# A two-layer hybrid decoder trunk: layer 1 loads its input in runs of 32 features and turns it in 32 by 32 blocks on VectorE

## The reference, cut to what matters

```python
def _rmsnorm(x, w):
    return x * lax.rsqrt(jnp.mean(x * x, axis=-1, keepdims=True) + EPS) * w

def _layer(x, ...):
    h = _rmsnorm(x, norm_w)
    z = jnp.einsum('btd,dc->btc', h, w_in)      # 1024 -> 3088 columns
    ...                                         # GLA and retention, per head norm, SiLU gates
    return x + jnp.einsum('btc,cd->btd', mixed, w_out), ...

for l in range(2):
    hp = _layer(hp, ...)                        # the prompt
y_prompt = _rmsnorm(hp, final_norm_w)
```

## Time and profile before

| | |
|---|---|
| median of 3 runs | 1725.38 us |
| the profiled execution's own time | 1724.93 us |
| its span | 1722.9 us |
| TensorE busy | 1701.6 us, 99% of the span |
| VectorE, ScalarE, GpSimd busy | 55%, 38%, 49% |
| DMA queues: ScalarE's (q10), SyncE's (q1) | 23.7%, 14.2% of 16 engines |
| granted TensorE clock | full over the span (0.999) |

### The profile page before, as it was taken

The page is one execution under the profiler, slowest core; times in us unless marked ns, Lnnn a source line. Parts: engine busy times, 40 slices in busy tenths (PEclk is TensorE's granted clock), DMA queues, the critical chain, the costliest instruction groups (busy, mean ns, idle before and its releaser), DMA issues.

```text
span 1722.9 us, 26529 instructions
## 1 busy us (share of the span) xinstructions
PE 1701.6 (99%) x10266; PEld 1401.0 (81%) x10266; DVE 942.0 (55%) x2284; ACT 657.6 (38%) x1287; POOL 842.1 (49%) x661
## 2 busy tenths in 40 slices
PE   6999999999999999999999999999999999999998
PEld 4888878888788887888878888788888888878886
DVE  7643566746555174464454535759556464584454
ACT  4433334333344234343452424434244343443322
POOL 4444345654455444464444544547445464454635
PEclk9999999999999999999999999999999999999999
DMA  7422356434442244322452224563244322442224
GB/s 259 135 65 84 100 207 197 147 111 145 161 137 84 86 135 159 117 86 83 136 168 88 74 74 149 184 178 128 74 150 159 111 76 85 134 157 80 86 86 140
DMA packets 100189, 215.97 MB, mean 125 GB/s; under 512 B 12896, under 2 KB 15328, under 8 KB 100064
## 3 DMA queue, kind: packets, MB, share of 16 engines
q10 hardware_dynamic: 73872, 134.51, 23.7%
q1 hardware_dynamic: 26192, 79.76, 14.2%
HBM read 192.34 MB, written 21.89 MB: 124 GB/s over the span
## 4 chain that ended last, share of the span: by engine, by line
PE 99%; DMA 1%; DVE 0%; issue 0%; ACT 0%; ACTq 0%; POOLq 0%; POOL 0%; SPq 0%
PE bank L697 82%; PE bank L972 2%; PE bank L1013 2%; PE bank L978 2%; PE bank L760 1%; PE bank L956 1%; PE bank L939 1%; PE bank L918 1%; PE bank L373 1%; PE bank L880 1%; PE bank L922 1%; PE bank L718 0%; PE bank L989 0%; PE bank L770 0%; PE bank L897 0%; PE bank L662 0%
## 5 line engine op out<-in xcount | busy, mean ns | idle before, releaser
L264 POOL TENSOR_TENSOR w_lo<-w_stage,w_hi 128x512 fp32r<-128x512 f32 x264 | 360.9, 1388 | 352.3 <-ACT w_hi L257 352.3
L697 PE MATMUL bank<-h_hi,w_hi 128*128 128x512 f32 x1024 | 410.2, 401 | 3.7 <-DVE h_lo L361 3.7
L697 PE MATMUL bank<-h_lo,w_hi 128*128 128x512 f32 x1024 | 400.4, 391 | 0.0
L697 PE MATMUL bank<-h_hi,w_lo 128*128 128x512 f32 x1024 | 400.2, 391 | 0.0
L264 POOL TENSOR_TENSOR w_lo<-ss,w_hi 128x512 fp32r<-128x512 f32 x164 | 216.5, 1341 | 232.4 <-ACT w_hi L257 232.4
L257 ACT ACTIVATE w_hi<-w_stage 128x512 fp32r<-128x512 f32 x264 | 152.6, 624 | 352.4 <-PE bank L697 311.0
L697 PEld LDWEIGHTS bank<-h_hi,w_hi 128*128 128x128 f32 x1024 | 192.7, 188 | 53.9 <-issue 7.2
L697 PEld LDWEIGHTS bank<-h_hi,w_lo 128*128 128x128 f32 x1024 | 192.8, 188 | 41.5
L697 PEld LDWEIGHTS bank<-h_lo,w_hi 128*128 128x128 f32 x1024 | 193.0, 189 | 37.0
L697 PE MATMUL bank<-w_hi,m_hi 128*128 128x512 f32 x512 | 203.6, 398 | 0.0
L697 PE MATMUL bank<-w_hi,h_hi 128*128 128x512 f32 x512 | 202.7, 396 | 0.0
(11 more groups left out here) (221 smaller groups left out, 2279.8 us busy)
## 6 DMA issues: line engine op xcount, KB each, us to landing
w_stage<-in_w_slots ACTq DMA_DIRECT2D x264, 256.0 KB, 3.0
ss<-in_w_slots ACTq DMA_DIRECT2D x164, 256.0 KB, 2.9
v_b<-in_w_slots ACTq DMA_DIRECT2D x84, 256.0 KB, 3.0
region<-in_x_prompt SPq DMA_DIRECT2D x32, 512.0 KB, 4.2
xn<-in_x_t SPq DMA_DIRECT2D x16, 512.0 KB, 4.3
out_acts<-region SPq DMA_DIRECT2D x16, 512.0 KB, 3.5
xn<-out_acts SPq DMA_DIRECT2D x16, 512.0 KB, 3.8
region<-out_acts SPq DMA_DIRECT2D x16, 512.0 KB, 3.4
```

Of the source, the lines that this page charges most:

```text
L264: pool.tensor_tensor(w_lo[:, r, c], stage(h), w_hi[:, r, c].bitcast(f32), ALU.subtract).then_inc(lo_done, 1)
L697: i = pe.matmul(P[q][:, :], x, y, start=(s == 0 and kk == 0 and c == 0), stop=(s == 3 and kk == 1 and c == 2), skip_group_check=True)
```

## The change

Layer 1 gets its input in the layout of layer 0. The load of `acts` is cut: for each 128 features (k) and each 32 of them (j) one DMA brings 32 tokens by 16 groups by 32 features, so that partition 32j + b holds, for each of 16 groups of 32 tokens, token b's 32 features (runs of 128 bytes). 32 DMAs of 64 KB (8 in each of windows 4 to 7) stand where 4 of 512 KB stood. In window 20 VectorE turns all 32x32 blocks in place with 4 `transpose` instructions of 128x1024 (`next_turned`, in place of `next_norm`). The factors come from layer 0's output rows while they are in SBUF: the `tile_stats` and `mean_square` at the end of a block now run in layer 0 too (into `yvar`), GpSimd makes `xrs_1` of them in window 2 of the next block, and `next_stats` and its `rsqrt` in windows 18 and 19 are gone. `scale_rows`, `next_scaled` and the short forms of `next_hi` and `next_lo` are used in both layers; `next_transpose` is gone.

```diff
+        xrs_1, yvar = sb("xrs_1", [128, NBLK, TPB]), sb("yvar", [128, TPB])
+        xb_in = Count(sem("xb_in"), 512, base=-512 * NBLK)
...
-        def next_norm(vec, m):
-            vec.wait_ge(rstd_x.sem, rstd_x.at(m, 1))
-            for t in range(TPB):
-                i = vec.tensor_scalar(xn[:, t, :], xn[:, t, :], xrs[:, t:t + 1], None, ALU.mult)
+        def next_turned(vec, m):
+            vec.wait_ge(xb_in.sem, xb_in.at(m, 512))
+            for k in range(0, KT, 2):
+                i = vec.transpose(x_t[:, k:k + 2, :], x_t[:, k:k + 2, :])
             i.then_inc(xn_sb.sem, 1)
...
         def next_hi(act, m, k):
-            act.wait_ge(ht_ps.sem, ht_ps.at(m, k + 1))
-            h4 = xn[:, :, 128 * k:128 * k + 128]
-            nc.scalar.activation(h4, (X if k % 2 == 0 else ATT)..., ACT.Copy, scale=nw[:, k:k + 1]).then_inc(h_sb.sem, 1)
             act.wait_ge(h_sb.sem, h_sb.at(m, k + 1))
-            nc.scalar.activation(h_hi[:, k, :].rearrange(...), h4, ACT.Copy).then_inc(hhi_sb.sem, 1)
+            nc.scalar.activation(h_hi[:, k, :], x_t[:, k, :], ACT.Copy).then_inc(hhi_sb.sem, 1)
...
-        def next_transpose(pe, m, k):
-            ...
         def scale_rows(pe, m):
-            if m > 0:
+            factor = xrs if m < NBLK else xrs_1[:, m - NBLK, :]
+            if m >= NBLK:
+                pe.wait_ge(rstd_y.sem, rstd_y.at(m - NBLK, 1))
+            elif m > 0:
                 pe.wait_ge(rstd_x.sem, rstd_x.at(m, 1))
...
         def next_scaled(vec, m, k):
-                if m > 0:
+                if m >= NBLK:
+                    vec.wait_ge(xn_sb.sem, xn_sb.at(m, 1))
+                elif m > 0:
                     vec.wait_ge(x_in.sem, x_in.at(m, 64))
...
             def load_next(m, t):
-                    sp.dma_start(xn[:, t, :], d["acts"][c:c + TOK, :]).then_inc(x_in.sem, 16)
+                    for k in (2 * t, 2 * t + 1):
+                        runs = d["acts"][c:c + BLK, 128 * k:128 * k + 128].rearrange("(c b) (j a) -> j b c a", b=32, a=32)
+                        for j in range(4):
+                            sp.dma_start(x_t[32 * j:32 * j + 32, k, :].rearrange("p (c a) -> p c a", a=32), runs[j]).then_inc(xb_in.sem, 16)
...
-                        if w == (8 if n < NBLK - 1 else 19) and n < LAST:
+                        if w == 2 and 0 < n <= NBLK:                       # GpSimd
+                            pool.wait_ge(ystat.sem, ystat.at(n - 1, 4))
+                            rsqrt(xrs_1[:, n - 1, :], yvar[:, :], rstd_y.sem)
+                        if w == 8 and n < NBLK - 1:
...
-                        if w == 27 and n < NBLK - 1:                       # TensorE: scale_rows
+                        if w == 27 and n < LAST:
...
-                        if 27 <= w < 31 and NBLK - 1 <= n < LAST:
-                            for k in (2 * (w - 27), 2 * (w - 27) + 1):
-                                ...
-                                next_transpose(pe, n + 1, k)
...
-                        if w == (2 if n == 0 else 1 if n < NBLK - 1 else 18) and n < LAST:   # VectorE
+                        if w == (2 if n == 0 else 1) and n < NBLK - 1:
                             next_stats(vec, n + 1)
                         if w == 20 and NBLK - 1 <= n < LAST:
-                            next_norm(vec, n + 1)
+                            next_turned(vec, n + 1)
...
-                        if w == 28 and n < NBLK - 1:
+                        if w == 28 and n < LAST:
                             next_scaled(vec, n + 1, 0)
                             next_scaled(vec, n + 1, 1)
...
-                        if w == 30 and l == DEPTH - 1:
+                        if w == 30:
                             vec.wait_ge(y_add.sem, y_add.at(n, 4))
                             for t in range(TPB):
                                 tile_stats(vec, y_t, t, (0,))
...
-                        elif q > 0 and l == DEPTH - 1:
+                        elif q > 0:
                             vec.wait_ge(y_add.sem, y_add.at(n, 4 + q))
                             tile_stats(vec, y_t, q - 1, (1,))
...
-                    elif l == DEPTH - 1:
+                    else:
                         vec.wait_ge(y_add.sem, y_add.at(n, 8))
                         tile_stats(vec, y_t, TPB - 1, (1,)).then_inc(ystat.sem, 1)
-                        mean_square(vec, ystat, n % NBLK)
+                        mean_square(vec, ystat, n, xvar if l == DEPTH - 1 else yvar)
```

More of the change, by code:

```diff
@@ L286, in tile_stats, with mean_square @@
             return i
[L288 removed]
+        def mean_square(vec, count, n, var=xvar):
             vec.wait_ge(count.sem, count.at(n, 1))
@@ L297, in mean_square @@
             vec.wait_ge(count.sem, count.at(n, 3))
-            vec.scalar_tensor_tensor(xvar[:, :], xms[:, :], EPS, xagg[:, :, 1], ALU.add, ALU.add).then_inc(count.sem, 1)
+            vec.scalar_tensor_tensor(var[:, :], xms[:, :], EPS, xagg[:, :, 1], ALU.add, ALU.add).then_inc(count.sem, 1)
         def tile_mean_square(vec, s, t):
@@ L328, in next_stats @@
         def next_stats(vec, m):
[L329 to L332, removed]
+            vec.wait_ge(rows_in.sem, rows_in.at(m, 64))
             for t in range(TPB):
-                i = tile_stats(vec, x_rows if m < NBLK else xn, t)
+                i = tile_stats(vec, x_rows, t)
             i.then_inc(xstat.sem, 1)
             mean_square(vec, xstat, m)
-        def next_norm(vec, m):
-            vec.wait_ge(rstd_x.sem, rstd_x.at(m, 1))
-            for t in range(TPB):
-                i = vec.tensor_scalar(xn[:, t, :], xn[:, t, :], xrs[:, t:t + 1], None, ALU.mult)
+        def next_turned(vec, m):
+            vec.wait_ge(xb_in.sem, xb_in.at(m, 512))
+            for k in range(0, KT, 2):
+                i = vec.transpose(x_t[:, k:k + 2, :], x_t[:, k:k + 2, :])
             i.then_inc(xn_sb.sem, 1)
@@ L347, in next_hi @@
                 act.wait_ge(nw_in.sem, nw_in.at(m, 16))
[L348 to L351, removed]
-            act.wait_ge(ht_ps.sem, ht_ps.at(m, k + 1))
-            h4 = xn[:, :, 128 * k:128 * k + 128]
-            nc.scalar.activation(h4, (X if k % 2 == 0 else ATT)[:, :].rearrange("p (t n) -> p t n", t=TPB), ACT.Copy, scale=nw[:, k:k + 1]).then_inc(h_sb.sem, 1)
             act.wait_ge(h_sb.sem, h_sb.at(m, k + 1))
-            nc.scalar.activation(h_hi[:, k, :].rearrange("p (t n) -> p t n", t=TPB), h4, ACT.Copy).then_inc(hhi_sb.sem, 1)
+            nc.scalar.activation(h_hi[:, k, :], x_t[:, k, :], ACT.Copy).then_inc(hhi_sb.sem, 1)
         def next_lo(vec, m, k):
             vec.wait_ge(hhi_sb.sem, hhi_sb.at(m, k + 1))
[L360 to L364, removed]
-        def next_transpose(pe, m, k):
[L367 to L374, removed]
+            vec.tensor_tensor(h_lo[:, k, :], x_t[:, k, :], h_hi[:, k, :].bitcast(f32), ALU.subtract).then_inc(hlo_sb.sem, 1)
         def scale_rows(pe, m):
-            if m > 0:
+            factor = xrs if m < NBLK else xrs_1[:, m - NBLK, :]
+            if m >= NBLK:
+                pe.wait_ge(rstd_y.sem, rstd_y.at(m - NBLK, 1))
+            elif m > 0:
                 pe.wait_ge(rstd_x.sem, rstd_x.at(m, 1))
@@ L382, in scale_rows @@
                     pe.wait_ge(first_rs, t // 2 + 1)
-                i = pe.transpose(ATT[:, TOK * t:TOK * t + TOK], xrs[:, t:t + 1].to_broadcast([128, 128]), ident[:, :])
+                i = pe.transpose(ATT[:, TOK * t:TOK * t + TOK], factor[:, t:t + 1].to_broadcast([128, 128]), ident[:, :])
             i.then_inc(ht_ps.sem, KT)
@@ L405, in load_next @@
             def load_next(m, t):
-                c = m % NBLK * BLK + t * TOK
+                c = m % NBLK * BLK
                 if m < NBLK:
@@ L660, in hT_slot0 @@
                                 r = slice(64 * hf + 32 * (k % 2), 64 * hf + 32 * (k % 2) + 32)
[L661 to L664, removed]
+                                i = pe.matmul(ATT[r, 0:256], wg[:, k, :], x_t[:, k, 256 * hf:256 * hf + 256], start=(k < 2), stop=(k >= 6))
                         i.then_inc(slot_used, 1)
@@ L1761, in body @@
                                 vec.tensor_tensor(y_t[:, q, 0:512], P[q][:, :], y_t[:, q, 0:512], ALU.add).then_inc(y_add.sem, 1)
-                        if w == 28 and n < NBLK - 1:
+                        if w == 28 and n < LAST:
                             next_scaled(vec, n + 1, 0)
                             next_scaled(vec, n + 1, 1)
-                        if 28 <= w < 31 and n < NBLK - 1:
+                        if 28 <= w < 31 and n < LAST:
                             next_scaled(vec, n + 1, 2 * (w - 27))
```

13 lines of the change are left out of this document (3 added, 10 removed).

## The result

The changed kernel takes 1712.58 us in the median of 4 runs (1712.16 to 1712.96), the kernel before on the same chip 1725.34 us (1724.88 to 1726.38). The ratio is 0.9925, with a 95% interval of 0.9908 to 0.9942: 12.8 us faster. The profiled executions say the same: spans of 1711.2 and 1722.9 us, 11.7 us apart, both at a granted clock of 0.999.

What follows compares the result with a forecast made beforehand. TensorE's time was taken as the only bound: 13.9 us removed, 1.8 added, 12.2 less taken, all other terms 0, so 1724.93 - 12.2 = 1712.7 us profiled, 1713.2 in the median; range 1711.0 to 1722.

Steps and rivals of the forecast that it cites:

- TensorE's own time: Blocks 3 to 6: 16 groups of 8 transposes go (13.9 us), four factor groups come (1.8 us); 12.2 us less taken.
- The loads: 32 DMAs of 64 KB per block in windows 4 to 7 delay weights, with cost 0 to the end.
- The additive price: A new load row, 2 KB in 16 runs, priced as bytes plus runs: 0.09 + 16 x 0.015 = 0.33 us.
- SyncE's queue: In block 5 `load_v`, behind window 7's DMAs, comes some 7 us later; VectorE idles 6.12 us there, the delay ends there.
- The turn: VectorE, windows 18 to 20: four turns of 1.3 us, 5.2 where 4.2 stood, covered by 9.14 us idle in block 3.
- The end of the block: Windows 27 to 32: layer 0's 2.46 us of statistics fit 2.9 us idle, else 6.5 us remain; cost 0.
- A: Weights starve if a packet costs 0.5 us or more: 1740 us in full (0.10), 1716 to 1728 in part (0.05).
- B: VectorE late at a block's end, past 6.5 us of cover: 2 to 3 us per block return, 1722 to 1726; chance 0.05.
- C: Turned input comes later than window 20, VectorE stands before the second scores: 1730 us and more; chance 0.03.

Runs made afterwards that it cites:

- the groups given back alone: The changed kernel with 8 identity transposes, read by nobody, behind each of slots 27 to 30 of blocks 3 to 6: 1726.75 us.
- the version that moves outputs: The changed kernel with the retention group's normed outputs turned by SyncE's DMAs and VectorE instead of TensorE: 1701.04 us.
- the one with more statistics: The changed kernel with sixteen unread bn_stats of 512 columns added to VectorE's queue at window 30 of blocks 0 to 6: 1721.46 us.

## Why the prediction was right

*TensorE's own time.* Forecast 12.2 us less, by groups 16 x 0.87 - 4 x 0.44 = 12.1, by blocks 12.0 to 12.4. Measured 12.4 from slot 0 to slot 0, 12.8 in the median of runs, 14.2 for the groups given back alone. One reading behind it is not exact: of the 16 groups removed 14 show 0.87 us in the chain of the kernel before and two, in block 5 right behind 32 small matmuls, show 1.02:

```profile
1278.44 1.02 PE bank L373 x8
```

The sum stands all the same, since block 5 is only 3.48 us longer with its four groups given back, as much as 4 x 0.87. This step is the whole result, and it rested on rows of the kernel before, because layer 0 already ran the new scheme.

*The loads.* The cost to the end was put at 0, and none can be told from the runs. The term behind it was mis-sized: I took 0.32 us for 2 KB in 16 runs, 20 ns a run; it is 12.8 ns, 0.205 us. So no backlog of 5.5 us built up, the weights' packets met shorter ones, and the sign that I named, ScalarE waiting for weights in windows 5 to 9 of blocks 3 to 6, up to 5 us at a time, is missing (0.4 us in block 3, nothing in the others): over the span it waits for weights 28.8 us in 15 places, 30.8 in 15 before. The estimate by the Trainium skill (DMA: Bandwidth & Descriptors), 30 us a block, would need 0.95 us of each DMA, which the page measured for a DMA that GpSimd issues; at 12.8 ns a packet one with 512 runs, issued by SyncE, takes 0.41 us of each engine. The additive price had counted every run of `load_v` in the earlier trace rows at 16 ns over its bytes. From 32 to 128 bytes the price rises from 8.9 to 12.8 ns, so by estimate some 8 ns belong to the packet and the rest to its bytes.

*SyncE's queue.* `load_v` did come later in block 5, 5.9 us by its distance from slot 0 (forecast 7). The prediction named only VectorE's idle time behind it and not that VectorE already waited for it before the change, 4.6 us; that wait is now 7.1 us, and TensorE's none. The runs of 32 bytes showed how right the place was and how near: when that queue is 54 us late, 43 arrive at the end.

*The turn.* 1.21 us each against 1.3, four in 4.61 us, 8.52 us idle behind them in block 3. What I had not seen is that block 4, with work in other shapes, has 6.6 us of cover there and not 9, still more than the turn added.

*The end of the block.* The four statistics did fit into the idle time ahead of the last low parts (2.90 us, now 0.52 left); those end at 651.90, 6.5 us before slot 0, as forecast. The true cover is 8.3 us there, for the two reasons shown above, and 6.8 us in block 0.

*The rivals.* A (weights starve) needed 31 ns a run and met 12.8; runs of 32 bytes, at four times the count, starved nothing either, since SyncE issues them no faster. B (VectorE late) is real as a mechanism, but decides only from some 7 to 8 us of further work at that place, three times the statistics that the change put there. C needed 100 us for the load, and moving it 12 windows later made VectorE wait 4.4 us, all hidden.

## What to carry to other kernels

Where one engine is the bound without a hole and the same kernel already holds a stretch without the work in question, read the gain from that stretch and spend the rest of the thought on what stands behind each moved step in its own queue. Turning a matrix by DMAs in runs of 128 bytes and 32 by 32 block transposes on an idle VectorE took 12.8 and then 15.0 us off a kernel that TensorE bounds, and it paid as long as nothing urgent stood behind the DMAs on the issuing engine or behind the turn on VectorE. Once TensorE waits, the bill can be larger than the wait: in one execution 2.8 us of it cost 3 more by the clock.

## What the runs showed of the hardware

- A run of 128 bytes from HBM to SBUF costs a DMA engine 12.8 ns, one of 32 bytes 8.9 ns, beside weights that stream at the same time (share of 16 engines, times the stretch, over the packets). Between two places in SBUF it is nearly the same, 12.3 ns, by the version that moves outputs (736 to 757 us):

```profile
q1 hardware_dynamic: 8160, 0.98, 29.8%
```

The Trainium skill (DMA: Bandwidth & Descriptors, section Why small descriptors are slow) says that transfers from SBUF to SBUF don't suffer from small packets. By that rule the second should be near the price of its bytes, by estimate 184 / 32 = 5.8 ns from the rows of 4 KB; here it is twice that, and 4% below the run from HBM.

- A subtraction of VectorE with two inputs took twice as long while GpSimd subtracted too: the two low parts at 649.36 to 651.90 took 2.54 us beside GpSimd's pair, and 1.27 us at 664.01, where GpSimd was idle until 668.49. GpSimd in the changed kernel, and then in the one with more statistics:

```profile
648.36 2.99 POOL L266 TENSOR_TENSOR w_lo<-w_stage,w_hi 128x512 fp32r<-128x512 f32 x2 [2.46 <-ACT w_hi L259]
```

```profile
668.49 2.56 POOL L266 TENSOR_TENSOR w_lo<-ss,w_hi 128x512 fp32r<-128x512 f32 x2 [6.38 <-ACT w_hi L259]
```

The Trainium skill (GPSIMD Engine Reference, section Specifications) has GpSimd and VectorE contend when VectorE reads two inputs; the trace agrees.

- In a wait of 2.8 us TensorE's clock fell to 1.2 GHz and stayed there for some 6 us of work behind it (above). In the wait of 43.1 us it fell too, and came back some 5 us after TensorE began again. In and after one of 2.7 us, in the kernel that turns three times, the granted clock stayed at 1.00 in the profiled run:

```profile
1009.00:1013.00 4.00, 1.28 (x11) 0.99 (x10) 2.84 (x5) 1.15 (x2) 2.50 (x2) 1.00 0.40 135
1013.00:1017.00 4.00, 4.00 (x41) 3.40 (x41) 2.48 (x11) 0.66 (x2) 0.00 (x0) 1.00 0.00 0
```

Its other three runs are 1.3 to 2.7 us longer at 0.997 to 0.998 against 0.999, which a fall of the clock in the same place would explain; no trace of them shows it.
